# Two RWKV layers on one core: modulation blocks issued in pairs inside the level steps

## The reference

```
m = silu(cond) @ w_mod + b_mod          # (1024,) @ (1024, 6144), split in 6: shifts, scales, gates
h = rmsnorm(x, g_pre_mix) * (1 + sc1) + sh1
q, k, v, r, k_rw, v_rw = project(h)     # h @ w_in
o = concat(attention(q, k, v), rwkv(r, k_rw, v_rw, ...)) @ w_o
x = x + gt1 * rmsnorm(o, g_post_mix)
h = rmsnorm(x, g_pre_ffn) * (1 + sc2) + sh2
x = x + gt2 * rmsnorm(ffn(h), g_post_ffn)   # dense SwiGLU in layer 0, top 2 of 8 experts in layer 1
```

## Time and profile before

| | us |
|---|---|
| median of 3 runs | 2561.65 (2556.39 to 2564.15) |
| profiled execution | 2558.78 |
| its span, first to last instruction | 2557.0 |
| TensorE busy | 2385.5 (93%) |
| weight loads busy | 2034.8 (80%) |
| VectorE busy | 1439.4 (56%) |
| ScalarE busy | 1120.9 (44%) |

### The profile page before, as it was taken

How to read it: one execution, slowest core, us unless ns; L and a number is a source line. 1 busy time by engine, 2 the same in 40 slices (tenths; PEclk the granted TensorE clock), 3 DMA queues, 4 the chain that set the end, 5 groups by cost and what they waited for, 6 DMA issues and landing times.

```text
span 2557.0 us, 66046 instructions
## 1 busy us (share of the span) xinstructions
PE 2385.5 (93%) x28817; PEld 2034.8 (80%) x28817; DVE 1439.4 (56%) x2662; ACT 1120.9 (44%) x2128; POOL 152.7 (6%) x174
## 2 busy tenths in 40 slices
PE   6998899998999999998999889988899999999995
PEld 3996677776789999896996677776688888888884
DVE  2246555555543333346246565656477777777787
ACT  3225555443432222124225555544444555555563
POOL 0002001100000000001001010110010000000011
PEclk8999999999999999999999999999999999999998
DMA  7225121122022222222221111110086677777783
GB/s 283 77 81 184 67 69 53 53 70 72 9 104 78 75 75 75 74 75 103 75 83 52 67 37 37 37 37 6 1 302 226 191 244 245 239 225 255 248 298 146
DMA packets 82328, 302.22 MB, mean 118 GB/s; under 512 B 9552, under 2 KB 9680, under 8 KB 81904
## 3 DMA queue, kind: packets, MB, share of 16 engines
q1 hardware_dynamic: 71072, 257.94, 30.9%
q0 software_dynamic: 10960, 39.98, 4.2%
HBM read 272.59 MB, written 25.30 MB: 116 GB/s over the span
## 4 chain that ended last, share of the span: by engine, by line
PE 69%; PEld 11%; DVE 10%; issue 4%; ACT 3%; DMA 1%; POOL 1%; SPq 0%; PEldq 0%; DVEq 0%; POOLq 0%; ACTq 0%
PE ps L520 10%; PE ps L521 10%; PE ps L522 10%; PE ps L1693 9%; PE ps L1278 6%; PE ps L1694 4%; PEld ps L520 4%; PEld ps L522 4%; PEld ps L521 3%; PE ps L874 2%; PE ps L533 2%; PE ps L994 2%; PE ps L1201 2%; PE ps L1037 2%; PE ps L1053 1%
## 5 line engine op out<-in xcount | busy, mean ns | idle before, releaser
L1693 PE MATMUL ps<-hg,w_ffn 128*128 128x512 f32 (+7 forms) x1408 | 411.3, 363 | 7.7 <-DVE ring_lo L2409 6.6
L2409 DVE TENSOR_TENSOR ring_lo<-ring,w_ffn 128x1024 fp32r<-128x1024 f32 x264 | 322.6, 1222 | 129.6 <-ACT w_ffn L1822 129.5
L1822 ACT ACTIVATE w_ffn<-ring 128x1024 fp32r<-128x1024 f32 x264 | 278.5, 1058 | 218.6 <-PE ps L1694 146.3
L1694 PE MATMUL ps<-hg,ring_lo 128*128 128x256 f32 (+7 forms) x1408 | 350.8, 249 | 0.0
L1693 PEld LDWEIGHTS ps<-hg,w_ffn 128*128 128x128 f32 x1408 | 265.0, 188 | 28.4 <-issue 10.0
L1694 PEld LDWEIGHTS ps<-hg,ring_lo 128*128 128x128 f32 x1408 | 268.5, 191 | 0.8
L1278 PEld LDWEIGHTS ps<-arena 64*64 64x64 f32 x7680 | 164.9, 135 | 84.9 <-issue 65.1
L522 PE MATMUL ps<-hT_ffn_hi,ring_lo 128*128 128x320 f32 x704 | 216.0, 307 | 0.0
L520 PE MATMUL ps<-hT_hi,w_proj 128*128 128x320 f32 x672 | 206.1, 307 | 7.1 <-DVE hT_lo L2415 7.1
L1278 PE MATMUL ps<-arena 64*64 64x64 f32 x7680 | 190.0, 222 | 21.3 <-issue 18.8
L521 PE MATMUL ps<-hT_lo,w_proj 128*128 128x320 f32 x672 | 208.5, 310 | 0.0
(11 more groups left out here) (393 smaller groups left out, 4958.7 us busy)
## 6 DMA issues: line engine op xcount, KB each, us to landing
ring<-in_blocks SPq DMA_DIRECT2D x484, 512.0 KB
h_rows<-arena POOLq DMA_DIRECT2D x16, 512.0 KB, 10.2
arena<-h_rows POOLq DMA_DIRECT2D x6, 1024.0 KB, 12.7
y_rows<-arena POOLq DMA_DIRECT2D x8, 512.0 KB, 5.6
x<-in_x_all SPq DMA_DIRECT2D x1, 2560.0 KB, 13.1
h_plain<-arena POOLq DMA_DIRECT2D x5, 512.0 KB, 8.5
out_y_all<-x POOLq DMA_DIRECT2D x5, 512.0 KB, 3.7
w<-in_low POOLq DMA_DIRECT2D x2, 768.0 KB, 6.6
```

The lines of the kernel that those rows point to most:

```text
L1693: nc.tensor.matmul(both, w_h[:, c], m[:, :, kc, 0:n], start=kc == 0, stop=False)
L1694: mm = nc.tensor.matmul(both[:, 0, :], w_l[:, c], m[:, 0, kc, 0:n], start=False, stop=kc == KC - 1)
L1822: A(high[:, n % slots, :], ring[:, n % RING, :], ACT.Copy).then_inc(*E.sig("w_hi"))
L2409: V.tensor_tensor(ring_lo[:, n % RING, :], ring[:, n % RING, :], high[:, n % high.shape[1], :], ALU.subtract).then_inc(*E.sig("w_lo"))
```

## The change

Only the table changes. Of a single group the blocks go from steps 4, 6, 8, 9 to 5, 5, 8, 8; of the two groups of unit 7 from 4, 4, 5, 6 and 6, 7, 8, 9 to 4, 4, 5, 5 and 7, 7, 9, 9. The steps of the copy and the turn stay.

```
@@ -741,7 +741,7 @@
         def mod_slots(g):

-            return [((4, 4, 5, 6), 7, 8), ((6, 7, 8, 9), 10, 11)] if len(mod_groups(g)) == 2 else [((4, 6, 8, 9), 10, 11)]
+            return [((4, 4, 5, 5), 7, 8), ((7, 7, 9, 9), 10, 11)] if len(mod_groups(g)) == 2 else [((5, 5, 8, 8), 10, 11)]
```

## The result

The changed kernel takes 2576.72 us (median of 8 runs, 2563.40 to 2584.57), the kernel before 2562.12 beside it (8 runs, 2556.39 to 2568.36). The ratio is 1.0067, interval 1.0046 to 1.0088: slower, by 14.6 us between the medians and 17 by the ratio. The forecast was 2559 and its range ended at 2570.

What follows compares the result with a forecast made beforehand. The prediction took TensorE, fed 256 instructions per 3.47 us, as the bound. Gains of 1.2 + 2.0 + 0.5 = 3.7 us, less a little for evictions, gave 3 us: median 2561.65 to 2559, range 2546 to 2570.

Steps and rivals of the forecast that it cites:

- What bounds the kernel: Dense 64x64 level work: TensorE can't be fed faster than 256 instructions in 3.47 us; up to 1.37 us other work free.
- 13.52 and 15.21: Microseconds per four-interval stretch, level 3 to products of y: without blocks, and with four; difference mostly put on ring transfers.
- Merging, the gross gain: Both scans over units: 25 fewer block places at 0.98 us each, 24.5 us less TensorE work.
- The transfers: Behind each pair in layer stretches: 1 MB bursts delay instruction packets; stretch 15.08 us, 1.2 us gained over nine units.
- 1.2 hits of 1.30 us: Late instruction packets that show per stretch, each costing 1.30 us over an undisturbed 3.47 us interval.
- nine stretches: Four-interval stretches of the nine single units that follow another unit's scan; 136.93 us in all before the change.
- the bounds (+3.5 and -8.2): Gain limits in us over nine units: one showing hit per unit, 14.82 us a stretch; two, 16.12.
- Units 0 and 8: Units with no scan beside the levels: early blocks precede VectorE waits, two later places become one; 2.0 us gained.
- The double unit: Unit with two groups: three places fewer, 2.9 us, but ring stays as busy; 0.5 us gained, bounds 0 and 2.
- Evictions: Steps 4, 6 and 9 lose the block covering ScalarE and VectorE emptying banks; cost 0, at most 3.4 us.
- the third, doubled bursts: Rival for the stretches: 2.5 packets a unit hit and showing, 16.77 us each, 11.5 us slower, 2573; chance 0.12.
- The signs named ahead: Profile signs for the forecast: x8 groups, "issue" stops up some 20 us, TensorE busy down 20 us or more, span hardly moved.

Runs made afterwards that it cites:

- e11: Kernel before, slots unchanged, with one added 512-column product after steps 7 and 10 of each single-group unit; ratio 0.9999 to before.
- e6: Changed kernel with only the second pair made, single groups at 4, 6, 8, 8 and unit 7 as before; ratio 1.0070 to before.
- e14: Kernel before, slots unchanged, second block's transfer asked for two steps later, third and fourth held to the next unit's token tiles; ratio 0.9969 to before.
- e10: Changed kernel, first pair's second transfer two steps later, second pair's held to the next unit's token tiles, unit 7's second transfers two steps later; ratio 0.9936 to before.
- e7: Changed kernel, slots unchanged, with the second transfer of each pair asked for two steps later; ratio 0.9997 to before.

## Why the prediction was wrong

Point by point, in its own order.

- **What bounds the kernel** was right, and the experiments rest on it. TensorE is fed in portions of 256 instructions, and work beside the feed is cheap: e11 adds 23 us, its stops at the edges are 11.4 us shorter (32.8 against 44.2), and the higher clock pays the rest. "Can't be fed faster than 256 instructions in 3.47 us" says too much: 3.47 is what they take in a row of such intervals, and the one ahead of such a row took 2.60 in unit 13 of before (1651.02 to 1653.62). Nor is all that lies between 13.52 and 15.21 the ring: in unit 3 two blocks fell into one interval, which took 4.12 us with TensorE busy throughout (444.98 to 449.10). That the sequencer's fetch of a block is "mostly hidden" (Trainium skill, Runtime: NRT & Kernel Launch, Instruction fetch mechanics) fits after even less than before: 63.1 us of stops at these edges.
- **Merging, the gross gain**: right in kind. All blocks run as x8, in 1.06 us at the full clock. The count of places was off by one (24, not 25). That hardly any of it would be on the path held as well.
- **The transfers** is the step that failed, in its size. I took 1.2 hits of 1.30 us in each of the nine stretches, and so a gain of 1.2 us in all; the nine stretches got 4.9 us longer. The mechanism was stated, 1 MB on end, longer than a feed interval, with no block behind it. But the price of a hit was taken as the mean of hits by small bursts. With 1 MB in flight a hit interval takes 5.10 to 5.45 us, so 1.6 to 2.0 above 3.47. The same nine stretches as in the earlier trace rows:

```profile
sum 141.87, PE 107.12 PEld 84.10 DVE 91.11 ACT 86.78 POOL 0.00; mean PE 11.90 PEld 9.34 DVE 10.12 ACT 9.64 POOL 0.00
```

  141.87 against 136.93: TensorE has 11.2 us less to do there and takes 4.9 longer. 15.76 a stretch, an excess of 2.24 over the floor of 13.52. At 1.9 a hit that is 1.2 hits, the number that I took; the price was wrong. The timeline agrees: eight of the nine stretches hold one interval of 5.1 to 5.5 us, where before one did. I had the bounds (+3.5 and -8.2) and took a value at the low end of them "because two of the four intervals now have the slack of no block to give", which is an argument for the high end: e6 shows what the missing block of step 9 costs.
- **Units 0 and 8**: 2.0 us gained was forecast. They got longer, 35.1 to 37.4 and 35.0 to 38.8 us. The waits at L1116 grew from 0.77 to 1.92 us, as the step said of taking blocks from in front of them. What it didn't say is that a wait of 2 us for VectorE is as long a stop as one for a packet (timeline of unit 0, answering to the earlier trace rows):

```profile
335.57 0.77 PE L1116 MATMUL ps<-con,arena 128*128 128x128 f32 x5 [1.92 <-DVE arena L2605]
341.27 0.77 PE L1116 MATMUL ps<-con,arena 128*128 128x128 f32 x5 [2.02 <-DVE arena L2605]
```

  Behind the wait that ended at 341.27 the clock is at the lower level from 348.1 to 351.5, and in unit 8 from 1488.1 and again from 1494.9, each for 3.4 us. Unit 8 shows it as a clock of 0.91; unit 14, where the long stop was a late packet (3.02 us), has 0.92. Both had 1.00 in before (rows of the two units of after):

```profile
1475.60:1514.35 38.75, 32.92 (x943) 26.18 (x942) 21.56 (x43) 18.38 (x46) 4.60 (x3) 0.91 0.16 57
1692.01:1732.71 40.70, 34.56 (x1080) 29.62 (x1079) 22.16 (x49) 18.05 (x44) 4.59 (x3) 0.92 0.16 55
```

- **The double unit**: half a microsecond gained was forecast; it grew by 2.2 us (27.86 to 30.09, from its start to the next L1201), though it has two places fewer. The reading of its stretch was wrong already: of the 18.27 us TensorE stood still for 2.27 only (0.26 and 2.01), nearly all of it in the last interval, so three of its four intervals of 4.57 were its own work and no sign of late packets.
- **Evictions** held. At the level line ScalarE and VectorE cost less than 2 us from 360 to 588 us, under the 5 us that would have spoken against the step. The waits of TensorE in that stretch, answering to the earlier trace rows:

```profile
PE ps L1278 <- issue: 12.8, 12, 2.5
...
PE ps L1278 <- ACT arena L2076: 0.9, 3, 0.3
PE ps L1278 <- DVE arena L2684: 0.8, 3, 0.3
```

- **A missing step: the granted clock.** No term of the sum has it, and it carries most of the loss. I had the earlier trace rows chosen at full clock, and priced every stop at its own length. But the page of before has a row with the clock, its units at 0.97 and 0.99, and two stops of over 2 us there already. By the fits, the change costs 1 to 3 us with the clock taken out, where 3 us of gain was forecast; the clock adds 8 to 13.
- **Of the rivals** it came out as the third, doubled bursts, given 0.12. Its time, 2573, is 4 us from the median; its mechanism was half right. It charged the whole 11.5 us to stretches of 16.77 us, and "stretches above 16 us" was its sign. Four of the nine are above 16 (16.40, 16.53, 16.55 and 16.15), their mean is 15.76. The stretch gave less than half of the loss. The rest is outside it: units 0 and 8, the double unit, and the clock.

The signs named ahead: all x8, right; stops up by some 20 us in the two scans, right (18.9); intervals of 4.6 us and more behind each pair, half right (one in eight of the nine stretches, so behind one pair of the two); busy time down by 20 us or more with the span hardly moved, wrong (7.4 down, 18.7 up), since the same work is busy for longer at 1.2 GHz (the 127 matmuls above: 5.12 us busy and 8.09). The sign should have named the sum of instructions by their length at full clock. The odd units of layer 1, forecast unchanged at 33.9, are 34.5, 34.7 and 34.9, up by 0.4 to 1.4 us.

## What to carry to other kernels

Look at the small instruction queue and at the granted clock before crediting a saving on TensorE: where its instructions arrive 256 at a time, work with few and long instructions is cover, and taking it away saved nothing here. Merging steps that consume streamed weights merges their transfers as well; ask for the second one later, or in a part of the kernel where TensorE has slack. Here that was worth 0.3% with the blocks as before (e14), and 0.3 to 0.6% with the pairs.

## What the runs showed of the hardware

- A load of 1 MB on end delays the instruction packet so far that 256 instructions take 5.10 to 5.45 us, against 3.47 in a row of intervals with nothing in flight and 4.57 to 5.10 beside the smaller bursts of before. With the second half megabyte asked for two steps later and the second pair's transfers held back (e10), the same stops went from 2.10 and 2.46 us to 0.50 and 1.64; with the halves spaced alone (e7), to 0.46 and 2.46.
- Stops of TensorE of 1.8 to 3.0 us were mostly (11 of 14 in after) followed by 3.4 or 6.8 us at 1.2 GHz, whether the stop was a late packet or a wait for VectorE; the same 127 matmuls took 8.09 and not 5.19 us. The undisturbed feed of the earlier trace rows, with stops of 0.71 to 1.38 us, was not followed by it.
- The mean granted clock of a run told its time to within a few us, 2.0 us for each 0.001, over 132 runs of one unchanged kernel. Runs of this one program differ by themselves, from 2545 to 2580 us. Between kernels the clock doesn't tell all: with the transfers well timed they were, by that slope, 3 to 10 us faster at the same clock.
